# Key and value halves of the compression products, with a linear between them

## What is computed

```python
def conv_mixer(a, state, w_in, w_conv, w_out):
    gb, gc, v = jnp.split(a @ w_in, 3, axis=-1)
    u = gc * v
    ...
    return (gb * conv) @ w_out, u_ext[:, t:]

def compress(rows, w_cmp):
    b, L = rows.shape[:2]
    nc = L // CMP_BLOCK
    blocks = rows[:, :nc * CMP_BLOCK].reshape(b, nc, CMP_BLOCK, N_KV_HEADS, 2, HEAD_DIM)
    return jnp.einsum('bnlgcd,lgcde->bngce', blocks, w_cmp)
```

## Time and profile before

| | us |
|---|---|
| median of 3 runs | 1374.5 |
| lowest and highest | 1374.09, 1375.25 |
| the profiled execution, its own time | 1377.6 |
| span of its instructions | 1375.9 |
| TensorE busy | 1278.7 (93%) |
| VectorE, ScalarE, GpSimd busy | 345.0, 268.6, 145.0 |
| mean granted clock of TensorE | 0.976 |

### The profile page before, as it was taken

The page is one execution under the profiler, slowest core; times in us unless marked ns, Lnnn a source line. Parts: engine busy times, 40 slices in busy tenths (PEclk is TensorE's granted clock), DMA queues, the critical chain, the costliest instruction groups (busy, mean ns, idle before and its releaser), DMA issues.

```text
span 1375.9 us, 36868 instructions
## 1 busy us (share of the span) xinstructions
PE 1278.7 (93%) x15542; PEld 1004.5 (73%) x15542; DVE 345.0 (25%) x1138; ACT 268.6 (20%) x710; POOL 145.0 (11%) x268
## 2 busy tenths in 40 slices
PE   7999999999999999999687878889999999999989
PEld 5878776777777776578343546687987978977967
DVE  2201102110111021002767673131211311311221
ACT  1000003000000012132866762020001001000020
POOL 3112211010000000232233340010000000000000
PEclk9999999999999999999988889889999999999999
DMA  9778688994450613463565776669879879779710
GB/s 315 296 265 305 244 322 200 259 348 148 180 177 0 252 57 138 146 109 94 184 210 166 240 241 226 235 246 357 324 295 395 310 304 398 300 303 391 296 57 31
DMA packets 107705, 322.12 MB, mean 234 GB/s; under 512 B 15400, under 2 KB 33641, under 8 KB 106388
## 3 DMA queue, kind: packets, MB, share of 16 engines
q1 hardware_dynamic: 90868, 263.71, 52.2%
q0 software_dynamic: 15520, 55.74, 14.1%
q10 hardware_dynamic: 1152, 0.30, 0.1%
HBM read 312.44 MB, written 14.52 MB: 238 GB/s over the span
## 4 chain that ended last, share of the span: by engine, by line
PE 88%; DVE 7%; ACT 3%; issue 2%; ACTq 0%; DVEq 0%
PE bank L1635 21%; PE bank L2136 17%; PE bank L1741 12%; PE bank L2147 8%; PE bank L1751 6%; PE bank L1694 5%; PE bank L2117 3%; PE bank L2104 2%; PE bank L1644 2%; PE bank L1791 2%; PE bank L1920 1%; PE bank L1763 1%; PE bank L1875 1%; PE bank L1914 1%; PE pbank L1860 1%
## 5 line engine op out<-in xcount | busy, mean ns | idle before, releaser
L2136 PE MATMUL bank<-X,gring 128*64 128x96 f32 x5632 | 236.0, 246 | 4.2 <-issue 3.8
L2136 PEld LDWEIGHTS bank<-X,gring 128*64 128x64 f32 x5632 | 233.3, 137 | 8.2 <-issue 8.2
L1635 PE MATMUL bank<-aT,gring 128*128 128x288 f32 x896 | 223.4, 407 | 6.9 <-DVE aT L1125 6.9
L1635 PEld LDWEIGHTS bank<-aT,gring 128*128 128x128 f32 x896 | 169.4, 190 | 55.0 <-issue 8.6
L1741 PE MATMUL bank<-aT,gring 128*128 128x288 f32 x704 | 171.0, 406 | 0.0
L1741 PEld LDWEIGHTS bank<-aT,gring 128*128 128x128 f32 x704 | 133.7, 190 | 36.9
L1164 DVE TENSOR_TENSOR hT<-hT,bank 128x288 f32<-128x288 f32 x96 | 39.3, 451 | 319.4 <-PE bank L2104 153.7
L2147 PE MATMUL bank<-Q,X 128*32 128x256 f32 x1728 | 96.4, 379 | 0.0
L1751 PE MATMUL bank<-Q 128*128 128x288 f32 x352 | 85.7, 406 | 0.0
L2147 PEld LDWEIGHTS bank<-Q,X 128*32 128x32 f32 x1728 | 55.4, 110 | 36.6
L1751 PEld LDWEIGHTS bank<-Q 128*128 128x128 f32 x352 | 66.9, 190 | 18.5
(11 more groups left out here) (287 smaller groups left out, 1210.8 us busy)
## 6 DMA issues: line engine op xcount, KB each, us to landing
gring<-in_moe SPq DMA_DIRECT2D x176, 512.0 KB, 5.7
Q<-in_moe SPq DMA_DIRECT2D x72, 512.0 KB, 7.2
gring<-in_dense_gu SPq DMA_DIRECT2D x44, 512.0 KB, 10.8
Q<-in_cache_cmp POOLq DMA_DIRECT2D x64, 256.0 KB, 5.8
Q<-in_cache_cmp SPq DMA_DIRECT2D x64, 256.0 KB, 5.7
gring<-in_conv_in SPq DMA_DIRECT2D x24, 512.0 KB, 10.4
Q<-in_dense_down SPq DMA_DIRECT2D x16, 704.0 KB, 5.0
gring<-in_ple_gate SPq DMA_DIRECT2D x16, 512.0 KB, 6.9
```

The costliest lines, as they stand in the source:

```text
L1635: ins = pe.matmul(bank(label, k)[:, 0:T], tile[:, 128 * i:128 * i + 128], rhs[:, i, :], start=i == 0, stop=i == C - 1)
L2136: ins = pe.matmul(bank(*part(i, M_GU + f))[64 * w:64 * w + 64, CAP * u:CAP * u + CAP], gslot(("m", 0), 2 * f + u)[:, o:o + 64], ae[:, c, : ...
```

## The change

The function that computed a whole compression now computes one half, and is called twice. In a block of the convolution the order becomes gc, v, ck, gb, cv; at the output linears (co, 3) comes between the halves of b = 6, and (co, 6) between those of b = 7. The list of results follows the same order. No other engine's program order changes.

```diff
     for c in range(C):
-        o += [("gc", c), ("v", c), ("gb", c)]
-        if c >= 2:
-            o += [("ck", c - 2), ("cv", c - 2)]
-    o += [("co", c) for c in range(3)] + [("ck", B - 2), ("cv", B - 2)]
-    o += [("co", c) for c in range(3, 6)] + [("ck", B - 1), ("cv", B - 1), ("co", 6), ("css", 0), ("css", 1)]
+        o += [("gc", c), ("v", c)] + ([("ck", c - 2)] if c >= 2 else [])
+        o += [("gb", c)] + ([("cv", c - 2)] if c >= 2 else [])
+    o += [("co", c) for c in range(3)] + [("ck", B - 2), ("co", 3), ("cv", B - 2), ("co", 4), ("co", 5)]
+    o += [("ck", B - 1), ("co", 6), ("cv", B - 1), ("css", 0), ("css", 1)]
...
-            def compress(b):
+            def compress(name, b):
                 if b == 0:
                     pe.wait_ge(wcmp_in, 16 * 4)
                 first, second = HALVES_OF[b % 3]
...
                     pe.wait_ge(c_in[k], 16 * 4 * (2 * (b // 3) + used + 1))
                     pe.wait_ge(c_pool_in[k], 16 * 4 * (2 * (b // 3) + used + 1))
...
             for c in range(C):
-                for name in ("gc", "v", "gb"):
-                    g_linear((name, c), aT, ready=0 if c == 0 and name == "gc" else None)
+                g_linear(("gc", c), aT, ready=0 if c == 0 else None)
+                g_linear(("v", c), aT)
                 if c >= 2:
-                    compress(c - 2)
+                    compress("ck", c - 2)
+                g_linear(("gb", c), aT)
+                if c >= 2:
+                    compress("cv", c - 2)
...
                 g_linear(("co", c), zT)
                 if c in (2, 5):
-                    compress(B - 2 + c // 5)
+                    compress("ck", B - 2 + c // 5)
+                elif c in (3, 6):
+                    compress("cv", B - 2 + c // 6)
```

More of the change, by code:

```diff
@@ L1686, in compress @@
                 low, apart = HALF_AT[first], HALF_AT[second] - HALF_AT[first]
-                for c, name in enumerate(("ck", "cv")):
-                    bank_free(pe, (name, b))
-                    for a in range(2):
-                        for l in range(16):
-                            for h in range(2):
-                                g = 2 * a + h
-                                src = bass.AP(Q[:, 0:1].tensor, low + 256 * c + 64 * g + 4 * l, [[QN, 128], [apart, 2], [512, 8], [1, 4]])
-                                ins = pe.matmul(bank((name, b))[64 * h:64 * h + 64, NB * a:NB * a + NB],
-                                                wc[:, 64 * c + 16 * g + l, :], src, start=l == 0, stop=l == 15)
-                    fill(ins, (name, b))
+                c = ("ck", "cv").index(name)
+                bank_free(pe, (name, b))
+                for a in range(2):
+                    for l in range(16):
+                        for h in range(2):
+                            g = 2 * a + h
+                            src = bass.AP(Q[:, 0:1].tensor, low + 256 * c + 64 * g + 4 * l, [[QN, 128], [apart, 2], [512, 8], [1, 4]])
+                            ins = pe.matmul(bank((name, b))[64 * h:64 * h + 64, NB * a:NB * a + NB],
+                                            wc[:, 64 * c + 16 * g + l, :], src, start=l == 0, stop=l == 15)
+                fill(ins, (name, b))
             pe.wait_ge(first_in, 16 * NFIRST)
```

## The result

The changed kernel took **1401.4 us** (median of 4 runs, 1394.46 to 1409.65), the kernel before beside it 1374.88 (4 runs, 1374.09 to 1380.12). The ratio is 1.0187, with a 95% interval from 1.0124 to 1.025. The forecast was 1385.5 with a range to 1393: the direction is right, the size is 2.4 times what was forecast, 26.5 us where 11 were expected. Two executions of the kernel before, among those taken beside the last experiments, took 2212 and 3351 us, count as slow and enter no ratio.

A forecast was written before the change was run, and what follows sets the result against it. TensorE was taken to bound the kernel, nearly unbroken until 210.69 us except for instruction-fetch stops. Terms summed to +8.9 us, 1383.4 from the median; with 2 us for the low clock the forecast was 1385.5, range 1380 to 1393.

The forecast's parts named there:

- stops vanish: Compressions two to eight: TensorE's instruction-fetch stops go, as a linear between halves lengthens each block; -12.6 us.
- waits for pages: Key halves of b=1 to 5 and 7: late pages needed one linear sooner, 1.7 to 3.1 us each; +15.2 us.
- key part of w_cmp: First key half: would start at 46.44, but the last part of its weights lands at 47.6; +1.2 us.
- weights of co 3: Fourth output linear, between the halves of b=6: due at 180.07, its weights land at 182.95; +2.9 us.
- ScalarE ahead of the squares: Before the squared-key products: value copy and one square no longer covered by an output linear; +1.05 us.
- borders: Small products after big ones start 0.14 us late; 16 such borders instead of 8; +1.1 us.
- low clock in the stage: Behind the new TensorE waits: one or two half-clock stretches of about 3.4 us; +2 us, bounds 0 and 17.
- The stops were instruction blocks: Inside compressions: TensorE stops where a fetched block of 127 records starts unloaded; a fetch takes 5.0 to 5.8 us.
- rival 4: Part of the delay is absorbed later, or landings come a little sooner; 1372 to 1377 us, chance 0.08.
- rival 2: Stops stay too, coming from something other than block length; +21.5 us, 1396 us, chance 0.05.
- Rival 1: Stops go and pages are not late, so the six waits vanish; -6.3 us, 1368.2 us, chance 0.07.
- rival 3: Low clock follows most waits, three to five stretches at 1.7 to 3.4 us more; 1389 to 1399 us, chance 0.15.

The follow-up runs named there:

- before_shift: Kernel before with 24 tiny matmuls (96 instructions) put ahead of the first linear; 1374.65 us in one run.
- keys_early: Changed kernel whose key half waits for and reads only the early half of its pages, twice (wrong keys); 1375.93 us, ratio 0.9978.
- pages_ahead: Changed kernel with the four page numbers of a late half read before the wait for the release; 1390.65 us, ratio 1.0074.
- after_again: The changed kernel itself, unedited, run and profiled once more; 1399.0 us, ratio 1.0146.
- tail_only: Kernel before with the change at the output linears alone (b=6 and b=7), convolution blocks in old order; 1383.44 us, ratio 1.0045.
- conv_only: Kernel before with the change in the convolution's blocks alone (b=0 to 5), output linears in old order; 1391.42 us, ratio 1.0096.
- pages_apart: Changed kernel, all page numbers read ahead, next sequence's early pages issued only once this one's late pages have landed; 1386.48 us, ratio 1.0079.
- warm: Changed kernel with 2 to 7 matmuls that nobody reads filling most of each TensorE wait; 1391.38 us, ratio 1.009.
- three_ahead: Changed kernel with five of a linear's products before the key half, three between halves, page numbers read ahead, w_cmp's key part awaited alone; 1371.03 us, ratio 0.9953.

## Why the prediction was right in its mechanism and wrong in its size

The growth of the stage in the first profiled execution is 212.67 - 195.39 = 17.3 us. Term by term:

| term | forecast | measured | from |
|---|---|---|---|
| stops vanish | -12.6 | -12.6 | no idle time inside a half |
| waits for pages | +15.2 | +15.8 | 2.34, 2.23, 2.71, 1.93, 2.63, 3.94 |
| key part of w_cmp | +1.2 | +1.2 | 1.22 |
| weights of co 3 | +2.9 | +2.8 | 2.79 |
| ScalarE ahead of the squares | +1.05 | +1.1 | 1.12 |
| borders | +1.1 | +3.3 | 0.35 a sequence, 2.7; and 0.07 at each of 9 waits |
| low clock in the stage | +2 | +5.6 | key halves of 5.33, 5.50, 5.42, 5.18 |
| sum | +10.9 | +17.2 | |

**The stops were instruction blocks: right.** Counting 127 records between stops gave the cause, and before_shift moved the stops to records named ahead. keys_early gained by the same removal with nothing else in the way. The Trainium skill (Runtime: NRT & Kernel Launch, Instruction fetch mechanics) says that crossing a block is mostly hidden. The seven stops of 1.01 to 1.82 us in before disagree, while the 127 records (254 instructions) between them agree with the size that it gives.

**The price of the pages: right.** Each wait came where it was said. The singles were off by up to 1 us either way (the second sequence 2.3 instead of 3.15, the eighth 3.9 instead of 2.9), the sum by 0.6. The same holds for w_cmp, co 3 and ScalarE. That the sum came out nearer than its parts is partly luck. Nothing was absorbed later (rival 4), and the stops did not stay (rival 2).

**Rival 1, faster because pages aren't late, is out, and so is an idea for making it true.** I had read the issues as half of the delay. pages_ahead took them away, 2.3 us for the second sequence, and the landing gained 0.7.

**The borders: too small.** A smaller step that failed is pricing a border only by the small products' late start, 0.14 us. A linear that stands alone costs too: 16 records take 4.08 us from start to start and 3.95 as a third of 48, and a wait takes 0.07 of overlap with it. The sum had 1.1, with 0 for the added waits; the rows say 2.7 and, with the waits, 3.3. The text's own bound for the added waits, 2.4 us more, would have covered it, but by another reckoning.

**The clock: the step that failed.** The text says of the waits "They stand between stretches of dense work, unlike the attention part where these rows come from, so I take one or two low stretches". That was not a reading: no row showed that dense work ahead of a gap protects from it. The profile has four low stretches after eight waits, 5.6 us; after_again has seven, 10.7 us. The text took 2 us. It also read the risk as lying in waits of 2.6 us and more; waits of 2.08 to 2.44 us were followed by the low clock as well. The warning of the Trainium skill on idle gaps (TensorE: Matmul & The Clock Gate, Why this matters for your kernels), which the text set aside, told what came: most of these waits were followed by 0.50 of the clock. They were shorter gaps than those which the page names, down to 2.08 us, and here the rows decide. The upper bound, 17 us for five waits and so 1400, lies near the measured 1401.4, but by luck: it took 3.4 us for each stretch, and one costs 1.2 to 1.7 in the change (2.7 once in tail_only). What the forecast had as rival 3, low clock after most waits, at a chance of 0.15, is what happened. Its 1389 to 1399 holds the profiled execution, 1394.46; the median is 2 us above it.

**The rest.** These terms explain the profiled execution: 1375.9 + 17.2 = 1393.1, and its span is 1392.8. The median of the four runs lies 7 us above its own time. The later profile of the same kernel shows low clock behind more of the same waits, which would do that. Of the other three runs of the first comparison only span and mean clock are known: 1397.3 at 0.967 to 1408.0 at 0.964, all under the 0.974 of the profiled one. Where in them the clock was lost is not shown. Beyond the stage it varies too: from the squared-key products on, the profiled executions of the study took 1162 to 1172 us, in no order that goes with the edits. So a difference of 2 or 3 us between two of these kernels rests on many runs, and not on one profile.

**What stays open.** Which wait is followed by the low clock. In one execution the waits of 1.93, 2.63 and 2.79 us were not and those of 2.23 and 2.34 were; in the other 2.08 was, twice. In the stage of six profiles (the two of the change, conv_only, tail_only, pages_ahead, pages_apart) 22 of the 27 waits of 2.08 to 4.19 us were followed by it. Three of the five that were not are the waits for w_cmp, of 2.12, 2.13 and 2.62 us; the wait for w_cmp was never followed by it. In warm it came behind two waits of 1.00 and 1.11 us with six records between them. The length of one idle time alone doesn't decide it, and no run here separates what else does.

## What to carry to other kernels

Moving a consumer earlier costs, for each time it runs, the slack that its transfer had, and slack must be read per transfer from the release to the landing: here 4 us were asked for and 1 to 2 were there, every round. A wait on TensorE is priced with what its clock does behind it, here 5.6 and 10.7 us on some 18 us of waits for pages and co 3, and that price is taken from rows that show an idle time and its clock, not from a reason why it might be spared. And where a run of small matmuls outruns the loading of instructions, few big ones between them can be enough: three of a linear's eight left 0.9 us of the 12.6, and moved the consumer by 1.5 us instead of 3.95.

## What the runs showed of the chip that I had not expected

- In the two profiles of the changed kernel most idle times of 2.08 to 2.82 us, between stretches in which TensorE worked without a break, were followed by 0.50 of the clock. The same kernel had four stretches of low clock in its stage in one execution and seven in another. Those of 2.63 and 2.79 us in the first profile were not.
- A stretch of low clock shows in the busy time, not in the idle time: TensorE's busy time rose by 4.9 us for the same 15542 matmuls (1278.7 to 1283.6), and a key half went from 3.95 to 5.50 us.
- Issuing four pages 2.3 us sooner let them land 0.7 us sooner, while the transfer engines were at 0.96 from 62 to 69 us at 344 GB/s; the last transfer took longer (7.0 us instead of 5.4).
- TensorE's stops lay two or three times 127 matmul records apart, to within two records, and all moved to the records named ahead when 96 instructions were put in front. 127 small records alone (3.8 us) weren't covered while the transfer engines were full, and six records of 288 columns among them (1.7 us) covered most of each: 0.9 us is left in three_ahead of the 12.6 in before.
